# Second block of a two-block transformer kernel: half output strips ahead of the last later sums, and another place for the pair norms' sums

## The reference, cut to what matters

```python
conv_out = _conformer_conv(c_val, c_gate, conv_w[l], conv_b[l], conv_ln_g[l], conv_ln_b[l])
attn_out = _stick_breaking(qkv[:, :, 0], qkv[:, :, 1], qkv[:, :, 2])
attn_out = _rmsnorm(attn_out, attn_norm_g[l]).reshape(B, S, SB_WIDTH)
mixed = jnp.concatenate([conv_out, attn_out], axis=-1)
y = jnp.einsum("bsc,cd->bsd", mixed, w_out[l])
h = h + _rmsnorm(y, g_post_mix[l])
...
# _conformer_conv ends in: y = _layernorm(y, ln_g, ln_b); return silu(y)
# _stick_breaking, for each head and each block of 128 queries:
log_beta = jax.nn.log_sigmoid(z)
log_1m_beta = jnp.where(mask, jax.nn.log_sigmoid(-z), 0.0)
between = lax.cumsum(log_1m_beta, axis=3, reverse=True) - log_1m_beta
attn = jnp.where(mask, jnp.exp(log_beta + between), 0.0)
return jnp.einsum("bhqk,bhkd->bhqd", attn.astype(vh.dtype), vh)
```

## Time and profile before

| | us |
|---|---|
| median of 3 executions | 1764.96 |
| lowest, highest | 1764.28, 1769.0 |
| the profiled execution | 1764.27 |
| its span in the profile | 1762.4 |
| mean granted TensorE clock | 0.996 |

### The profile page before, as it was taken

One profiled execution on the slowest core, in us unless ns is written; L12 is line 12 of the kernel. 1 busy time (PEld: TensorE's weight loads), 2 busy tenths in 40 slices (PEclk: granted clock), 3 DMA queues, 4 the chain that ended last, 5 costly groups with the idle time before them and its releaser, 6 DMA issues.

```text
span 1762.4 us, 21518 instructions
## 1 busy us (share of the span) xinstructions
PE 1722.1 (98%) x8215; PEld 1412.7 (80%) x8215; DVE 1257.3 (71%) x1915; ACT 819.2 (46%) x1345; POOL 38.0 (2%) x87
## 2 busy tenths in 40 slices
PE   8999999999999999999999999999999999999998
PEld 7887888888888777778888888788788788888886
DVE  6666358687888667765778788888987544765766
ACT  7433244343445656764433443632768532333342
POOL 0000000000001121000000000000000000000000
PEclk9999999999999999999999999999999999999999
DMA  7222442333412112116142423033100353224212
GB/s 250 84 72 84 127 136 76 117 97 106 137 43 64 61 50 71 37 49 190 48 145 71 132 76 116 13 107 96 49 13 5 92 179 96 72 87 143 68 49 84
DMA packets 195749, 158.29 MB, mean 90 GB/s; under 512 B 5248, under 2 KB 161280, under 8 KB 195648
## 3 DMA queue, kind: packets, MB, share of 16 engines
q1 hardware_dynamic: 194240, 154.16, 28.9%
q0 software_dynamic: 400, 1.25, 0.3%
q10 hardware_dynamic: 1008, 1.53, 0.3%
HBM read 154.81 MB, written 2.10 MB: 89 GB/s over the span
## 4 chain that ended last, share of the span: by engine, by line
PE 89%; DVE 6%; ACT 3%; issue 1%; DMA 0%; POOL 0%; DVEq 0%; SPq 0%; ACTq 0%
PE ps L1060 29%; PE ps L1062 28%; PE ps L1061 28%; PE ps L1563 1%; PE ps L1130 1%; ACT sb L2019 1%; DVE sb L2236 1%; ACT sb L1762 1%; PE ps L1453 0%; DVE sb L2493 0%; DVE sb L2234 0%; DVE sb L2262 0%; PE ps L1189 0%; DVE sb L2729 0%; ACT sb L1768 0%
## 5 line engine op out<-in xcount | busy, mean ns | idle before, releaser
L1060 PE MATMUL ps<-sb,sb 128*128 128x512 f32 (+3 forms) x2435 | 930.4, 388 | 8.3 <-ACT sb L2019 5.2
L1062 PE MATMUL ps<-sb,sb 128*128 128x512 f32 (+3 forms) x2435 | 911.7, 379 | 0.0
L1061 PE MATMUL ps<-sb,sb 128*128 128x512 f32 (+3 forms) x2435 | 911.3, 379 | 0.0
L2236 DVE TENSOR_TENSOR sb<-sb,sb 128x1024 fp32r<-128x1024 f32 (+1 forms) x414 | 405.2, 998 | 218.8 <-ACT sb L1762 218.0
L1060 PEld LDWEIGHTS ps<-sb,sb 128*128 128x128 f32 (+1 forms) x2435 | 450.9, 188 | 111.1 <-issue 13.1
L1762 ACT ACTIVATE sb<-sb 128x1024 fp32r<-128x1024 f32 (+1 forms) x414 | 349.7, 871 | 394.2 <-PE ps L1062 389.3
L1062 PEld LDWEIGHTS ps<-sb,sb 128*128 128x128 f32 (+1 forms) x2435 | 450.5, 188 | 86.9
L1061 PEld LDWEIGHTS ps<-sb,sb 128*128 128x128 f32 (+1 forms) x2435 | 451.2, 188 | 81.9 <-issue 0.2
L2476 DVE TENSOR_TENSOR sb<-sb,sb 128x1024 fp32r<-128x1024 f32 x70 | 85.6, 1222 | 47.5 <-ACT sb L1924 45.2
L1919 ACT ACTIVATE sb<-sb 128x512 f32<-128x512 f32 x64 | 40.3, 631 | 130.8 <-DVE sb L2528 130.8
L2458 DVE TENSOR_TENSOR sb<-sb,sb 128x1024 f32<-128x1024 f32 x80 | 95.2, 1219 | 0.6
(11 more groups left out here) (217 smaller groups left out, 1111.4 us busy)
## 6 DMA issues: line engine op xcount, KB each, us to landing
sb<-in_w_up SPq DMA_DIRECT2D x86, 512.0 KB, 4.1
sb<-in_w_down SPq DMA_DIRECT2D x86, 512.0 KB, 4.8
sb<-in_w_gate SPq DMA_DIRECT2D x22, 512.0 KB, 4.0
sb<-in_a_w_in SPq DMA_DIRECT2D x20, 512.0 KB, 3.8
sb<-in_w_in SPq DMA_DIRECT2D x20, 512.0 KB, 3.8
sb<-in_w_o SPq DMA_DIRECT2D x16, 512.0 KB, 3.8
sb<-in_w_mem_kv SPq DMA_DIRECT2D x8, 512.0 KB, 7.6
sb<-in_w_out SPq DMA_DIRECT2D x8, 512.0 KB, 3.9
```

The source lines that it names most:

```text
L1060: mm(ps, lh, rh, start=start, stop=False, **k)
L1061: mm(ps, lh, rl, start=False, stop=False, **k)
L1062: return mm(ps, ll, rh, start=False, stop=stop, **k)
L2236: tt(lo, raw, hi, ALU.subtract).then_inc(S("w_lo"), parts)
```

## The change

Three things change in the list, all in the second block.

1. The product of the output strips 0, 1 and 2 with inner part 4 (`oa`, nine matmuls) is taken out of the steps `o` and put ahead of the later sums of unit 7; the product with inner part 5 stays where the whole strips stood.
2. Values of unit 6 come right behind these later sums, ahead of the sums of the layer norm's variance.
3. The pair norms' sums move: those of pairs 0 and 1 from the passes 4 and 6 into the convolution groups 0 and 2, behind their sixth tap (passes 3 and 5); those of pair 2 from right behind the later sums of unit 7 to right ahead of the values of unit 7, with `pr` and `px` of the pair. They wait for `keep` 7 instead of 6, and the values that wait for their reading are now those of unit 7, not 6.

```diff
-        if u >= 4:
-            PLAN_C += [("pt" if u % 2 else "ps", u // 2 - 2)]
+        if u >= 4 and u % 2:
+            PLAN_C += [("pt", u // 2 - 2)]
...
         PLAN_C += [BEHIND[u]]
+        if u in (3, 5):
+
+            PLAN_C += [("ps", u // 2 - 1)]
...
-    PLAN_C += [("bt", 7), ("ln_qa", 3), ("ps", 2), ("ln_var",), ("va", 6), ("ex", 7), ("pr", 2), ("ln_rs",), ("px", 2),
-               ("ah", 7), ("ln_mul", 0), ("at", 7), ("kp", 6), ("ln_mul", 1), ("o", (0, 1)), ("va", 7), ("silu", 0), ("ll", 0),
+    PLAN_C += [("oa", (0, 1, 2)), ("bt", 7), ("ln_qa", 3), ("va", 6), ("ln_var",), ("ex", 7), ("ln_rs",), ("ah", 7), ("ln_mul", 0),
+               ("at", 7), ("kp", 6), ("ln_mul", 1), ("o", (0, 1)), ("ps", 2), ("pr", 2), ("px", 2), ("va", 7), ("silu", 0),
+               ("ll", 0),
                ("o", (2,)), ("pt", 2), ("kp", 7), ("ps", 3), ("silu", 1), ("ll", 1), ("o", (3,)), ("silu", 2), ("pl", 2),
...
-    PAIR_SUMS = {4: 1, 2: 0, 6: 2}
+    PAIR_SUMS = {4: 1, 2: 0, 7: 2}
...
+        def pair_sums(p):
+            q.wait_ge(S("pair_sq"), p + 1)
+
+            q.wait_ge(S("keep"), 7 if p == 2 else 2 * p + 2)
+            for t in range(4):
+                m = mm(banks[6][:, 2 * t:2 * t + 2], OQ[:, 128 * t:128 * t + 128], HALF[:, :], start=True, stop=True)
+            m.then_inc(S("pair_ps"), 1)
...
+                if g in (0, 2) and k == taps[5]:
+                    pair_sums(g // 2)
...
+        def out_part(tiles):
+
+            held[:] = next_slab()
+            _, wh, wl = held
+            q.wait_ge(S("sb_exp"), 21)
+            for t in tiles:
+                k, a = OUT_KS[0][0], slice(128 * t, 128 * t + 128)
+                mixed_ready(k)
+                mm3(banks[t][:, :], M2h[:, k, a], M2l[:, k, a], wh[:, 0:512], wl[:, 0:512], True, False)
```

More of the change, by code:

```diff
@@ L1611, in block_step @@
                 out_first(a[0])
-            elif kind == "ps":
-                q.wait_ge(S("pair_sq"), a[0] + 1)
-                q.wait_ge(S("keep"), 2 * a[0] + 2)
-                for t in range(4):
-                    m = mm(banks[6][:, 2 * t:2 * t + 2], OQ[:, 128 * t:128 * t + 128], HALF[:, :], start=True, stop=True)
-                m.then_inc(S("pair_ps"), 1)
+            elif kind == "ps" and a[0] >= 2:
+                pair_sums(a[0])
+            elif kind == "oa":
+                out_part(a[0])
             elif kind == "pt":
@@ L1657, in out_strip @@
             return strip(w, OUT_KS[j], t, 4 * n + t, M2h, M2l, mixed_ready, j == 0, j == 3)
+        def out_part(tiles):
[6 more added lines that the diff above has]
+                mm3(banks[t][:, :], M2h[:, k, a], M2l[:, k, a], wh[:, 0:512], wl[:, 0:512], True, False)
         def out_first(tiles):
-            if not held:
-                held[:] = next_slab()
             for t in tiles:
-                q.wait_ge(S("sb_exp"), 21 if t < 3 else 24)
-                m = out_strip(held, 0, 0, t)
-                if t == 3:
-                    m.then_inc(S("w_used"), 1)
+                if t < 3:
+                    _, wh, wl = held
+                    k, a = OUT_KS[0][1], slice(128 * t, 128 * t + 128)
+                    mixed_ready(k)
+                    mm3(banks[t][:, :], M2h[:, k, a], M2l[:, k, a], wh[:, 512:1024], wl[:, 512:1024], False, False)
+                else:
+                    q.wait_ge(S("sb_exp"), 24)
+                    out_strip(held, 0, 0, t).then_inc(S("w_used"), 1)
         def out_slab(n, j, tiles):
```

## The result

| | before | after |
|---|---|---|
| median of 13 executions each, same chip | 1766.2 | 1771.37 |
| lowest, highest | 1764.28, 1769.05 | 1766.12, 1772.99 |
| the profiled execution | 1764.27 | 1770.99 |
| its span, its mean granted clock | 1762.4, 0.996 | 1769.2, 0.993 |

The ratio is 1.0024 with a 95% interval of 1.0017 to 1.0031, which is 4.2 us more (3.0 to 5.5); the medians of the table are 5.2 apart, the means 4.5. So the change costs a little. It lies about inside the 0.3% that the prediction took for what can be told from no change, and with 13 executions each it can be told.

What follows compares the result with a forecast made beforehand. TensorE, busy 1722.1 of 1762.4 us, was taken to bound the kernel. Terms 0.35 + 2.5 + 1.54 = +4.4 on the profiled 1764.27 gave 1768.7, stated as 1769.0 because the median was higher; range 1766.2 to 1771.5.

Steps and rivals of the forecast that it cites:

- Waits in the convolution groups: Groups 0 and 2: TensorE waits 0.55 and 0.75 for ScalarE's squared rows ahead of the moved sums of pairs 0 and 1.
- Low clock of pass 4 taken as gone: Later sums of pass 4: with the small matmuls moved away, the clock no longer falls, 1.54 less; bounds 0 and 1.54.
- a fall where TensorE is dense: Sign of being wrong: the granted clock falls in a stretch where TensorE is dense; no size given.
- Nine matmuls ahead of the later sums: Ahead of unit 7's later sums: 2.1 of products hidden in idle time, chain 0.35 shorter, later sums 0.25 sooner.
- The chain T to the sums of pair 3: From the start of unit 7's later sums to pair 3's sums: 17.9 against 15.37, 2.5 more, with waits 1.4, 2.4, 2.6.
- One fall on the path behind it: Behind the sums of pair 3: one clock fall lying on the path, 1.54 more; bounds 0 and 3.1.
- The base: Whole kernel: profiled execution 1764.27 plus 4.4 gives 1768.7; median of three 0.7 higher, so 1769.0 was said.
- the rival: Two clock falls on the path where one was counted; against it, falls half inside idle time cost nothing; chance 0.25.
- Rival 1: Last steps: no fall of the clock on the path, +2.9, 1767.2; chance 0.15.
- rival 2: Two clock falls, layer norm's transposes to first `os` strips, or pass 4's fall staying: +5.9, 1770.2 to 1771.8; chance 0.25.
- Rival 3: Last steps: VectorE reads pair sums 2.4 earlier, ScalarE reaches pair 3's squares 2.6 earlier: −1.9, 1762.6; chance 0.08.
- Rival 4: Last steps: ScalarE stands still for 1.4 around the table load, now on the chain: 1770.4; chance 0.02.

Runs made afterwards that it cites:

- the new order: Changed kernel with last steps reordered again: remaining half strips cover the layer norm's round trip, norms of pairs 2 and 3 behind all Silus; 1765.82, ratio 0.9996.

## Why the prediction was right, and where it was not

The difference was forecast at +4.4 and is +4.2 (3.0 to 5.5). The waits behind the later sums and their chain were right. That the total fits so well is luck: two terms of 1.54 failed and cancelled, as the steps show. By its steps:

1. **Waits in the convolution groups** 0.55 and 0.75: measured 0.40 and 0.59 (0.33 and 0.60 in the second execution). Right in kind, and 0.15 too long. But the sums themselves hold TensorE longer in the groups than the 0.81 booked: 0.91 to the next start, and some 0.3 more in the starts around them. So, beyond the 1.46, the logits of unit 4 came 1.59 later, and pass 5 added 1.75, where 1.36 and 1.56 were forecast.
2. **Low clock of pass 4 taken as gone, −1.54.** This step failed: in the first trace after, it is there (1292.5 to 1295.5 at 0.50, the 20 matmuls 4.61 long). In the second it is not. I had ascribed it to the small matmuls ahead of it, and over all 14 traces there is something in that: the seven with these sums in pass 4 all have 0.50 there, for 3.4 or 6.8 us, and of the seven with the sums moved two have it. But three of those seven have another stretch at 0.50 in pass 6 instead, and none of the seven others has (three of these have one in pass 5). In mean clock the move gave +0.0008 (alone), +0.0005 (with the order of the change) and −0.0001 (with the new order), in time +0.6, +0.7 and +1.6 us. A likelihood, which I had booked in full, and the gain in clock did not pay for the waits that came with it. It is also one of my own signs of being wrong, a fall where TensorE is dense: it was busy for 3.00 of 3.00 us there. With this step, the later sums of unit 7 start 2.13 later and not 0.35.
3. **Nine matmuls ahead of the later sums**, hidden, 0.25 less for ScalarE's earlier Exp: as said, with 0.26 by the landmarks (logits of unit 6 to the later sums of unit 7, 21.33 before and 21.07 after). The idle time ahead of them is 1.23 and not under 1. Only that the idle time of 2.76 was worth 1.54 of clock as well was wrong: four other traces have that idle time, and 3.3 for the 20 matmuls behind it.
4. **The chain T to the sums of pair 3**, 17.9: measured 17.93 and 17.92. All three waits stand where they were put, for whom they were put: 1.4, 2.4, 2.6 forecast; 1.41, 2.00, 0.89 in the first trace, 1.41, 0.51, 1.07 in the second. The first is untouched by the clock. The second was taken 0.4 too long: in the first trace TensorE ran at full clock ahead of it. For the rest, the last wait in both traces and the second in the second trace are smaller by what the low clock adds to TensorE's own work in front of them.
5. **One fall on the path behind it, +1.54.** The low clock came where it was named (between 1350 and 1366), but cost nothing there, since it lay in work that ends in a wait. I had written "half of a fall inside an idle time costs nothing" only against the rival. Two terms of 1.54 with opposite signs both failed, and that kept the sum: 0.35 + 2.5 + 1.54 was forecast, 2.13 + 2.56 + 0.11 came.
6. **The base.** The level 1769.0 was 2.4 under the median measured, though the difference was right, because the sum stood on an execution of 1764.27 at clock 0.996. Only 17 of the 91 had that clock, and the mean of all is 1766.6. A median of three said 1764.96, 1.2 under the median of 13. The addition was off too: 1768.7 and 0.7 are 1769.4, and the levels of the rivals were counted partly from 1764.27 and partly from 1769.0. The measured 1771.37 is above the forecast's own range (1767.8 to 1770.2), among the levels given to two falls, and 0.13 inside the whole range.

Rival 1 (no fall on the path, +2.9) had the better mechanism for the last steps. Of rival 2 the case "the fall of pass 4 stays" came true in one of the two traces, but the sum of rows did not come to its +5.9, as the fall in the last steps cost nothing. Rival 3, a gain, is refuted: VectorE's reading comes 11.90 behind the later sums (12.0 forecast), and the squares of pair 3 behind Silu 0. Rival 4 is refuted: the load starts 0.02 after `px` ends (1357.71 + 0.63 = 1358.34) and Silu 0 starts 0.01 after its end (1358.36 + 1.28 = 1359.64), with nothing else to wait for.

The rule of the Trainium skill (ScalarE: Activation LUTs, What ACT_TABLE_LOAD costs) gives 1283 ns for the load, and the trace agrees with 1.28 us. Its 1380 ns for draining the engine do not show in the trace, which has 0.02 us ahead of the load and 0.01 behind it.

## What to carry to other kernels

Work moved into one idle time is cover taken from another: name for each round trip of the other engines what TensorE does meanwhile, and walk their queues row by row; that chain came out at 17.93, 17.92 and 17.92 us in three traces, with 17.9 forecast, and taking one wait away brought up another. Cost a low clock only where TensorE's work does not end in a wait, and never book it to one cause from one trace. Where executions of one program differ by more than the change, take several, note each one's mean granted clock, and ask whether the base execution is a typical one.

## What was not expected of the hardware

The granted clock in stretches of short matmuls is not set by the program alone. One and the same program, the kernel before, had 0.50 in the later sums of unit 7 in one execution and full clock there in the other. It also differs where nothing was changed, in the first block. The stretch from 700 to 750 us, first of the kernel before in its first execution, then in its second:

```profile
700.00:750.00 50.00, 43.52 (x283) 34.12 (x283) 38.00 (x101) 32.66 (x83) 5.48 (x8) 1.00 0.16 47
```

```profile
700.00:750.00 50.00, 43.93 (x269) 35.08 (x271) 35.83 (x92) 31.47 (x80) 5.31 (x7) 0.93 0.13 43
```

A mean of 0.93 over 50 us is about 7 us at 0.50, and the logits of unit 0 start 2.24 later in the second (1238.07 against 1235.83). The first trace of the changed kernel has 0.93 there too, which is its offset of 1.46; its second has 1.00. Nor does TensorE have to stand still ahead of it: in pass 4 it was busy without a gap when the clock fell. Why one execution falls where another does not, no run here shows. And the clock is a better scale than it looks: over 206 executions of twelve programs its mean to three places takes out half of the scatter.
